# Hybrid decoder trunk on one core: fourteen weight loads of the gating unit cut at partition 120, and a mended entry in the table that places weights

## What is computed

```
def layer_c(h, w_in, v_norm, w_spatial, b_spatial, w_out):
    z = gelu(h @ w_in)                 # w_in: 1024 x 4096
    u, v = split(z, 2)
    v = rmsnorm(v, v_norm)
    mixed = w_spatial (causal) applied over 128 positions + b_spatial
    return (u * mixed) @ w_out

def peer(h, w_q, subkeys, u_tab, v_tab):
    q = h @ w_q                        # 8 heads x 2 halves x 128
    scores = q . subkeys               # top 16 of 128 in each half, then top 16 of the 256 sums
    idx, gate = ...                    # 128 experts for each token
    act = gelu(x . u_tab[idx])
    return sum(gate * act * v_tab[idx])
```

## Time and profile before

| | us |
|---|---|
| median of 3 runs (1626.75 to 1628.21) | 1627.13 |
| the profiled execution, its own time | 1626.47 |
| its span, first to last instruction | 1624.7 |
| PE busy | 1436.0 (88%) |
| DVE busy | 980.4 (60%) |
| ACT busy | 666.4 (41%) |
| POOL busy | 657.2 (40%) |
| data moved | 629.72 MB, 388 GB/s over the span |
| granted clock of TensorE, mean share of full speed | 0.987 |

### The profile page before, as it was taken

One profiled execution on the slowest core, in us unless ns is written; L12 is line 12 of the kernel. 1 busy time (PEld: TensorE's weight loads), 2 busy tenths in 40 slices (PEclk: granted clock), 3 DMA queues, 4 the chain that ended last, 5 costly groups with the idle time before them and its releaser, 6 DMA issues.

```text
span 1624.7 us, 14850 instructions
## 1 busy us (share of the span) xinstructions
PE 1436.0 (88%) x4450; PEld 705.9 (43%) x4450; DVE 980.4 (60%) x2487; ACT 666.4 (41%) x1841; POOL 657.2 (40%) x535
## 2 busy tenths in 40 slices
PE   7999989998777999998887999899989888897786
PEld 6646466653222434443342545355335344342222
DVE  1216658776778656643356855566456777777654
ACT  1515534443345335332244533343334453544434
POOL 1002324454554334343335434323334544546672
PEclk9999999999999999999999999999999999999999
DMA  5434999999999999999999999999999999999995
GB/s 210 173 138 158 421 345 400 406 411 421 420 422 421 421 421 421 422 421 422 422 421 421 420 418 421 422 420 419 422 421 418 423 420 422 419 421 421 421 421 217
DMA packets 87088, 629.72 MB, mean 388 GB/s; under 512 B 9808, under 2 KB 9952, under 8 KB 10720
## 3 DMA queue, kind: packets, MB, share of 16 engines
q0 software_dynamic: 73728, 536.90, 79.9%
q1 hardware_dynamic: 13104, 91.60, 13.8%
q10 hardware_dynamic: 176, 0.28, 0.1%
HBM read 627.69 MB, written 1.05 MB: 387 GB/s over the span
## 4 chain that ended last, share of the span: by engine, by line
PE 41%; DMA 38%; DVE 9%; issue 5%; ACT 4%; POOL 3%; SPq 0%; POOLq 0%; DVEq 0%; ACTq 0%
DMA ring<-in_peer_uv,experts 37%; PE acc L1568 21%; PE work L1355 5%; PE work L1338 5%; DVE ring L1217 5%; POOL ring L674 3%; PE work L1327 3%; PE acc L1531 1%; ACT diag L866 1%; PE work L1422 1%; PE work L1370 1%; ACT gelus L864 1%; DMA weights<-in_peer_w_q 1%; PE work L1550 1%; DMA weights<-in_ab_w_in 1%
## 5 line engine op out<-in xcount | busy, mean ns | idle before, releaser
L1568 PE MATMUL acc<-ring,diag 128*128 128x512 f32 x2048 | 977.2, 610 | 164.5 <-ACT diag L866 160.9
L674 POOL DMA_INDIRECT ring<-in_peer_uv,experts x512 | 647.7, 1265 | 852.8 <-PE acc L1568 716.8
L1217 DVE CUSTOM_DVE_ANT_0 ring<-ring,h 128x1024 f32<-128x1024 f32 x512 | 625.3, 1227 | 439.1 <-DMA ring<-in_peer_uv,experts 427.6
L1568 PEld LDWEIGHTS acc<-ring,diag 128*128 128x128 f32 x2048 | 366.9, 191 | 697.5 <-ACT diag L866 356.4
L863 ACT ACTIVATE gelus<-dots 128x1 f32<-128x1 f32 x512 | 102.9, 201 | 676.7 <-DVE dots L1217 676.0
L866 ACT ACTIVATE diag<-ident,gelus 128x128 f32<-128x128 f32 x512 | 205.6, 402 | 16.7
L864 ACT ACTIVATE gelus<-gelus,gates 128x1 f32<-128x1 f32 x512 | 150.8, 294 | 16.6
L1338 PE MATMUL work<-weights,hT 128*128 128x512 f32 x288 | 134.3, 596 | 0.0
L1355 PEld LDWEIGHTS work<-hT,weights 128*128 128x128 f32 x704 | 86.9, 195 | 22.7 <-issue 22.7
L1355 PE MATMUL work<-hT,weights 128*128 128x128 f32 x704 | 88.5, 278 | 5.8 <-issue 5.8
L1338 PEld LDWEIGHTS work<-weights,hT 128*128 128x128 f32 x288 | 54.8, 192 | 66.2 <-issue 66.1
(11 more groups left out here) (198 smaller groups left out, 840.3 us busy)
## 6 DMA issues: line engine op xcount, KB each, us to landing
weights<-in_c_w_in SPq DMA_DIRECT2D x25, 1024.0 KB
weights<-in_peer_w_q SPq DMA_DIRECT2D x14, 1024.0 KB
weights<-in_ab_w_in SPq DMA_DIRECT2D x10, 1024.0 KB
ring<-in_peer_uv,experts POOLq DMA_INDIRECT x512
weights<-in_c_w_out SPq DMA_DIRECT2D x6, 1024.0 KB
z<-in_c_w_out SPq DMA_DIRECT2D x6, 1024.0 KB
z<-in_peer_w_q SPq DMA_DIRECT2D x5, 1024.0 KB
weights<-in_ab_w_out SPq DMA_DIRECT2D x4, 1024.0 KB
```

Of the source, the lines that this page charges most:

```text
L674: pool.indirect_dma_start(ring[:, t % SLOTS, :], None, uv_rows, bass.IndirectOffsetOnAxis(ap=experts[:, b, step:step + 1], axis=0))\
L1217: nc.vector.tensor_tensor_reduce(out=ring[:, k, 0:D], in0=ring[:, k, 0:D], in1=h[:, b, :], scale=1.0, scalar=0.0, op0=ALU.mult, op1=ALU.ad ...
L1568: last = nc.tensor.matmul(acc[2 * b + n][:, :], diag[:, k, :], ring[:, k, D + n * CH:D + (n + 1) * CH], start=False, stop=True, skip_group ...
```

## The change

Each first half of a chunk of ZPROJ that is loaded (fourteen of them; halves that are kept in their room are not) is issued as two transfers, one of partitions 0 to 119 and one of partitions 120 to 127, both counted on the room's semaphore, whose numbers rise by two. The rest of the loads stay as they are. In the table, the rooms of WOUT's two chunks now count as used until the OUT stage that reads them last; before, until WOUT's own place.

```
--- before.py
+++ after.py
@@ -93,6 +93,7 @@
 LOW_ROOMS = ((0, 1), (2, 3))
 SCORES_ROOM, Z_HIGH_ROOM, Z_LOW_ROOM = 4, 5, 6
 N_ROOMS = 7
+MOST_ROWS = 120
 TK_PARTS = 6
 
 
@@ -290,6 +291,7 @@
         spans[room] = [(last_mix[0], places["ZTAKE", 1, Z_ORDER[1][0]]), (last_mix[1], len(PLAN))]
     kept = {("ZPROJ", 1, 3): ("ZPROJ", 0, 3), ("ZPROJ", 1, 2): ("ZPROJ", 0, 2), ("QPROD", 1, 1, 3, ALL): ("QPROD", 1, 0, 3, ALL)}
     kept_halves = {("ZPROJ", 0, 3): (0, 1), ("ZPROJ", 0, 2): (0,), ("QPROD", 1, 0, 3, ALL): (0, 1)}
+    in_two = []
     used_until, fills, pinned, homes = [-1] * N_ROOMS, [0] * N_ROOMS, set(), {}
     rooms, numbers, fresh = [], [], []
     for kind, args, at in walk():
@@ -300,7 +302,7 @@
             for half in range(2):
                 if uses is None:
                     room, wait = 2 * (n % 2) + half, "used"
-                    used_until[room] = places[name]
+                    used_until[room] = places["OUT", 1, i, 3] if kind == "WOUT" else places[name]
                 elif name in kept and half in kept_halves[kept[name]]:
                     room, wait = homes[kept[name]][half], None
                     pinned.discard(room)
@@ -321,8 +323,10 @@
                     free_from, room = max(choice, key=lambda c: c[1]) if forced else min(choice)
                     wait = "used" if used_until[room] == free_from else "span"
                     used_until[room] = end
+                split = bool(wait) and kind == "ZPROJ" and half == 0
                 if wait:
-                    fills[room] += 1
+                    fills[room] += 2 if split else 1
+                in_two += [(len(rooms), half)] if split else []
                 place.append(room)
                 number.append(fills[room])
                 new.append(wait)
@@ -332,10 +336,10 @@
             numbers.append(number)
             fresh.append(new)
             homes[name] = place
-    return rooms, numbers, fresh
-
-
-ROOMS, FILLS, LOADS = weight_rooms()
+    return rooms, numbers, fresh, in_two
+
+
+ROOMS, FILLS, LOADS, IN_TWO = weight_rooms()
 HALVES = {}
 for _stage in PLAN:
     if (_stage[0] == "ZMORE" and _stage[3] == 1) or (_stage[0] == "OMORE" and _stage[3] in (1, 3, 5)):
@@ -545,7 +549,10 @@
                         sp.wait_ge(*filled(max(BANKS["MIXT", block, k] for k in range(4))))
                     elif LOADS[n][half] and room in room_used:
                         sp.wait_ge(*room_used[room])
-                    if LOADS[n][half]:
+                    if (n, half) in IN_TWO:
+                        for rows in (slice(0, MOST_ROWS), slice(MOST_ROWS, P)):
+                            sp.dma_start(wide_rooms[room][rows], src[rows, 4 * half:4 * half + 4, :]).then_inc(chunk_in[room], 16)
+                    elif LOADS[n][half]:
                         sp.dma_start(wide_rooms[room], src[:, 4 * half:4 * half + 4, :]).then_inc(chunk_in[room], 16)
                     room_used[room] = used[half]
 
```

## The result

The changed kernel takes **1687.39 us** (median of 4, 1682.04 to 1688.38), the kernel before on the same chip 1626.94 (4 runs, 1625.21 to 1628.21): a ratio of 1.0364, 95% interval 1.0343 to 1.0384. It is 60 us slower; forecast were 1613.3 us, and 0.05 for slower. The profiled execution took 1682.04 us, span 1680.3.

A forecast was written before the change was run, and what follows sets the result against it. From 366 us on the sixteen DMA engines' bytes were taken as the bound. From 1626.47 us, 7.8 (Part A), 0 (Part B) and 5.6 (Part C) were subtracted to give 1613.1, stated as 1613.3; range 1609.5 to 1621.5.

The forecast's parts named there:

- What bounds the kernel: From 366 us on, DMA bytes at 418 to 423 GB/s; only when queues fill and how evenly engines finish move the end.
- Part A: Room table at the first streamed query chunk: earlier loads remove PE's 5.83 us stop; gain 7.8 us, bounds 4.9 to 9.5.
- Rival 3: The gain at the query chunk is not kept while the cut works: 1620.9 us, chance 0.05.
- Part B: Room table at ZPROJ 0, 2: a new PE stop of 5.2 to 5.5 us, covered by queued transfers, costing nothing.
- Rival 4: The new PE stop at ZPROJ 0, 2 is not covered: 1621.0 us, chance 0.05.
- Part C: The fourteen cut loads: one engine relieved of 35 us work, eight given 4.4 us each; gain 5.6 us, bounds 5.3 to 8.1.
- rival 1: The cut spreads over all sixteen engines, or the late engine is an untouched one: 1618.7 us, chance 0.16.
- If the relieved one is the late one: At the kernel's end: if the cut relieves the engine finishing 9.7 us behind the fifteenth, those 9.7 us go entirely.
- rival 2: The late engine takes an extra row, costing 4.4 us: 1623.1 with Part A, chance 0.10; 1630.9 without, 0.04.

The follow-up runs named there:

- the mend alone: Changed kernel with no load cut, every load one transfer of 128 partitions, only the room table changed: 1618.28 us, 0.9949 of the kernel before.
- the mend with and without it: The mend alone, 1618.28 us, against the same with ZPROJ 0, 2's first half put in room 1, which removes the new PE stop: 1619.05 us.
- 64: Changed kernel with its cut loads in parts of 64 and 64 partitions: 1671.67 us, ratio 1.0277 to the kernel before.
- the probes: The mend alone plus 24 unread last-pass loads, partitions in steps of 4: 1618.66 us (one row), 1619.10 (two), 1626.45 (four), 1626.44 (eight).

## Why the prediction was wrong

**What bounds the kernel** was right as far as it went: from 366 us on time is bytes. It then priced every row of every transfer at this rate, 0.31 us, and asked only how many rows each engine gets. The rate can change too, and did.

**Part A** was right in mechanism and size: the stop is gone, the group takes 1.95 us at 201.10, the windows from 215 us stand at 415 to 424, and the mend alone gives 7.8 us where 7.8 were taken. By the interval of its ratio the gain is 5.5 to 10.9 us, so that the two agree to a tenth is luck; the bounds of 4.9 to 9.5 are what held. Rival 3 is refuted.

**Part B** was right: 5.58 us of stop against 5.2 to 5.5, 3.78 against 1.88 us behind it, cost nothing. In the changed kernel the stop is 10.96 us, since the cut load itself lands 14.8 us after its issue, and uncut in the mend alone 9.8. Rival 4 is refuted by the mend with and without it.

**Part C** is the step that failed, and in two places. The first made the sign. "It loses 14 x 8 x 0.31 = 35 us of work, the eight gain 14 x 0.31 = 4.4 us each" priced only shares. The condition "if the cut works as its numbers suggest" held for the shares (the markers show fifteen and eight) but not for the 0.31 us. In the kernel before a row takes that long. Cut by partitions, the rows of both queues take 0.51 to 0.53 us, some 250 GB/s for all engines together, while the load is under way: -5.6 us forecast, about +69 measured, 3.6 us for each large part beyond its bytes and 1.3 for each small one. The rows of before could not show it, as every load of weights there and every gather names all 128 partitions. But the forecast's bounds for C, 5.3 to 8.1 us, held only gains, and the one loss among the rivals was 4.4 us; no cost of the transfer itself was put down, and no reason was given for leaving it out.

The Trainium skill (SBUF: State Buffer, "Door 1: The DMA port swizzle") says that the bandwidth of a transfer depends on how many of 16 ports its partitions reach. By that list 120 to 127 reach two ports and 0 to 63 reach eight, in line with the losses of the small part and of 64. Partitions 0 to 119 still reach all sixteen, so for the large part the list would give a loss only by what the engines hold at one moment, and the forecast never asked which partitions each engine would hold. The Trainium skill's "Don't bother" on two transfers to disjoint halves (DMA: Bandwidth & Descriptors, "Rules for kernel authors") stood in rival 1 at no cost; measured, the cut costs 3.1 to 4.9 us a load.

The second is "If the relieved one is the late one", which the prediction itself called its weakest step. By the probes the late one takes the third or fourth share of a transfer, so it was not relieved, and it was one of the eight that got a row more. The mechanism of rival 2 was thus the true one of those listed, but it priced 4.4 us; its 1623.1 misses the 1687 by as much as the rest. By the probes, 14 rows on that engine would cost some 4.4 us even without the slow packets (an estimate: 14/24 of 7.4 to 8.2). The 0.85 for faster rested on A being safe and on C costing at most 4.4 us.

Two sums of the prediction are off and change nothing: 1613.1 and 0.66 make 1613.7 and not 1613.3, and 1602 + 4.4 is 1606.4 and not 1606.6.

## What to carry to other kernels

Beside a full queue of gathers, cut a load of 128 partitions across its columns, if at all, and not across its partitions: the same 14 loads cost 2 us one way and 69 the other. A full DMA share says that the engines are occupied, not that they move bytes: read it with GB/s, and read the rate just behind the issue of the transfer in question. And before relieving "the late engine", find it: a few spare rows, on one engine more from run to run, in a stretch where nobody reads them, narrowed it here to two of sixteen.

## What was not expected of the hardware

- A load of eight rows of 8 KB moves the end by 1.47 us on partitions 120 to 127 and by 0.34 us on partitions 0, 4, 8 up to 28 (35.3 and 8.2 us over 24). The 0.34 is near the one row that the late engine gets, 0.31; the 1.47 is lost by the whole core.
- A load of 120 partitions lowers both queues together to 250 GB/s from 421, at a share of 1.01. Fourteen of them cost 50.5 us beyond their bytes in the middle of the kernel and 48 in the last pass.
- One engine is some 10 us behind the fifteen at the end, and 24 rows more on it move the end by 7.4 to 8.2 us; on the two lowest engines they move it by 0.4 and 0.8. The Trainium skill (DMA: Bandwidth & Descriptors, "Latency and other measured facts") names 7 and 15 as usually the slower ones. Here it is the third or fourth share, which by the same page ("Why a DMA increments its semaphore by 16 and not by 1") is engine 2 or 3. What gives it more to do stays open. The page of the profile has two queues of instruction packets, q8 with 0.57 MB and q14 with 0.37 MB; if one engine moved all of one of them, that would be 22 or 14 us at 26.3 GB/s (an estimate), but no view names their engines.
